# Seven half products in place of eight in the up-projections of a gated convolutional MLP

## The reference, cut to what matters

```
def _conv_ffn(h, w_up, conv_w, conv_b, w_down):
    u = h @ w_up
    up = jnp.pad(u, ((0, 0), (1, 1), (0, 0)))
    u = up[:, :-2] * conv_w[0] + up[:, 1:-1] * conv_w[1] + up[:, 2:] * conv_w[2] + conv_b
    a, v = jnp.split(u, 2, axis=-1)
    return (jax.nn.silu(a) * v) @ w_down
```

## Time and profile before

| | |
|---|---|
| median of 3 runs | 4205.89 us (4193.66 to 4224.21) |
| profiled execution, its own time | 4208.8 us |
| its span, first to last instruction | 4207.0 us |
| share of the span: PE / DVE / ACT / POOL busy | 88% / 52% / 25% / 20% |
| mean granted TensorE clock | 0.953 of 2.4 GHz |
| layer 0's up-projections | 2733.9 to 3188.8 us |
| layer 1's up-projections | 3741.35 to 4045.8 us |

### The profile page before, as it was taken

One profiled execution on the slowest core, in us unless ns is written; L12 is line 12 of the kernel. 1 busy time (PEld: TensorE's weight loads), 2 busy tenths in 40 slices (PEclk: granted clock), 3 DMA queues, 4 the chain that ended last, 5 costly groups with the idle time before them and its releaser, 6 DMA issues.

```text
span 4207.0 us, 52931 instructions
## 1 busy us (share of the span) xinstructions
PE 3699.3 (88%) x21315; PEld 2076.3 (49%) x21315; DVE 2204.5 (52%) x4437; ACT 1050.0 (25%) x2777; POOL 828.1 (20%) x892
## 2 busy tenths in 40 slices
PE   7988898999987998777777777699999998899999
PEld 4555665898855543233332332555554444444444
DVE  4846534787556666776776754623331037533311
ACT  1422221444222333322323322311110022411100
POOL 1034301444201334333333342000000000000000
PEclk8989998899888999999999999899999999999999
DMA  4145520000028999999999998211110111012212
GB/s 165 48 189 226 218 83 8 3 3 3 2 86 305 407 416 420 420 420 420 420 420 420 421 419 355 97 40 48 52 60 35 55 44 60 1 61 80 75 60 75
DMA packets 179573, 751.44 MB, mean 179 GB/s; under 512 B 12215, under 2 KB 74946, under 8 KB 104321
## 3 DMA queue, kind: packets, MB, share of 16 engines
q0 software_dynamic: 77264, 549.79, 31.7%
q1 hardware_dynamic: 101488, 196.16, 13.1%
q10 hardware_dynamic: 576, 2.10, 0.1%
HBM read 745.90 MB, written 2.10 MB: 178 GB/s over the span
## 4 chain that ended last, share of the span: by engine, by line
PE 57%; DMA 19%; DVE 9%; ACT 3%; issue 1%; POOL 0%; DVEq 0%; POOLq 0%; ACTq 0%; SPq 0%
PE bank L104 28%; DMA row<-in_experts,idxs 14%; PE bank L2739 9%; PE bank L2473 6%; DMA wring<-in_experts,idxs 4%; PE bank L2430 2%; PE bank L978 1%; DVE row L2665 1%; PE bank L959 1%; PE bank L1703 1%; PE bank L1677 1%; PE bank L1693 1%; DVE wring L2665 1%; DVE TT L1026 0%; PE bank L2997 0%
## 5 line engine op out<-in xcount | busy, mean ns | idle before, releaser
L2473 PE MATMUL bank<-row,dg 128*128 128x512 f32 x1444 | 692.1, 620 | 208.9 <-ACT dg L2572 208.6
L104 PE MATMUL bank<-h2T,wring 128*128 128x512 f32 (+1 forms) x2112 | 759.3, 522 | 0.0
L2665 DVE CUSTOM_DVE_ANT_0 row<-row,bank 128x1024 f32<-128x1024 f32 x361 | 440.9, 1221 | 305.1 <-DMA row<-in_experts,idxs 285.2
L104 PEld LDWEIGHTS bank<-h2T,wring 128*128 128x128 f32 x2112 | 402.6, 191 | 355.4 <-issue 337.1
L2473 PEld LDWEIGHTS bank<-row,dg 128*128 128x128 f32 x1444 | 272.5, 196 | 593.8 <-issue 580.8
L2723 POOL DMA_INDIRECT row<-in_experts,idxs x361 | 345.8, 958 | 620.1 <-PE bank L2473 553.4
L2739 PE MATMUL bank<-wring,gT 128*128 128x512 f32 x880 | 383.1, 598 | 8.6 <-DVE gT L3137 8.6
L2473 PE MATMUL bank<-wring,dg 128*128 128x512 f32 x604 | 294.3, 621 | 72.7 <-ACT dg L2572 72.6
L3126 DVE TENSOR_SCALAR cv<-pad,fp 128x769 f32<-128x769 f32 (+1 forms) x88 | 54.2, 616 | 509.1 <-ACT pad L3092 509.1
L104 PE MATMUL bank<-hT,wring 128*128 128x256 f32 (+1 forms) x864 | 283.9, 489 | 3.7 <-ACT sq L773 3.0
L2739 PEld LDWEIGHTS bank<-wring,gT 128*128 128x128 f32 x880 | 168.5, 192 | 221.0 <-issue 221.0
(11 more groups left out here) (545 smaller groups left out, 5111.4 us busy)
## 6 DMA issues: line engine op xcount, KB each, us to landing
wring<-in_ada_w SPq DMA_DIRECT2D x36, 2048.0 KB, 8.3
wring<-in_ffn_w_up SPq DMA_DIRECT2D x44, 1024.0 KB, 7.6
wring<-in_peer_w_query SPq DMA_DIRECT2D x16, 1024.0 KB, 9.8
wring<-in_ffn_w_down SPq DMA_DIRECT2D x8, 2048.0 KB, 7.8
wring<-in_w_in SPq DMA_DIRECT2D x7, 2048.0 KB, 8.1
wring<-in_ffn_w_down SPq DMA_DIRECT2D x4, 1536.0 KB, 6.7
wring<-in_attn_w_qkv SPq DMA_DIRECT2D x3, 2048.0 KB, 7.8
row<-in_experts,idxs POOLq DMA_INDIRECT x361, 24.7
```

The costliest lines, as they stand in the source:

```text
L104: ins = e.matmul(out, l, r, start=(start and n == 0), stop=(stop and n == len(pairs) - 1))
L2473: ins = e.matmul(ks[half], self.dg[u % 4], self.places[self.slot[u]][:, 1024 + half * 512:1536 + half * 512], start=(x == 0), stop=(x == 127))
L2665: e.tensor_tensor_reduce(row, row, P.pairs[g % 2], 1.0, 0.0, MUL, ADD, self.dots[:, g % 2, x:x + 1]).then_inc(*V.up("pg_dot", j))
```

## The change

Each pair of parts is treated as a 2 x 2 block product: the two rows of blocks are the `a` and the `v` part, the inner index is split into channel chunks 0 to 3 and 4 to 7, and the tokens are split into two halves (384 and 384 in layer 0, 256 and 256 in layer 1). Eight half products (four chunks over half of the tokens) become seven, with sums ahead of them and behind them (Strassen's scheme in Winograd's form):

- GpSimd forms four sums of weight blocks for each pair, each [128, 4, 128], that is 128 partitions x 512 elements: S3 = A11 - A21, S1 = A21 + A22 (written over A21 in the ring), S2 = S1 - A11, S4 = A12 - S2. S2 and S3 have two buffers, S4 one.
- VectorE forms four sums of token blocks once for each layer (T1 to T4, each [128, 4, 384] or [128, 4, 256]); T2 is written over a part of `h2T`.
- TensorE forms the products in the order 1, 5, 7, 6, 2, 3, 4, each of four matmuls over 384 or 256 tokens, each into a bank of its own.
- ScalarE copies product 1 into the pad of the first part; VectorE adds products 6, 7, 5, 7, 2, 3 and 4 to the pads (one SBUF and one PSUM operand), in 11 instructions in layer 0 (the context's edge cuts four of the adds in two) and 7 in layer 1. The convolution, Silu and `gT` are as before, for a pair at a time. There are two pads for each part of a pair.
- GpSimd issues the four DMAs of the convolution's weights ahead of its `begin`, and clears the four pads (after S2 of pair 0).
- The gate rows are made after the products (`mod_row`), and kept ahead of the last convolution (`keep_row`); their memory is shared with S2 and S3.
- `project` waits, chunk by chunk, only for those `gT` that it reads.

The core of the diff:

```diff
+    def products_pe(self, pe, p):
+        P, name = self.P, self.name
+        wb = self.slots[p // 2][1]
+        a11, a12, a22, s1 = [self.part(wb, p, *rc) for rc in ((0, 0), (0, 1), (1, 1), (1, 0))]
+        for n, lhs, rhs, needs in ((1, a11, self.B11, ()),
+                                   (5, s1, self.T1, (("T1",), ("S1", p))),
+                                   (7, self.S3[p % 2], self.T3, (("T3",), ("S3", p))),
+                                   (6, self.S2[p % 2], self.T2, (("T2",), ("S2", p))),
+                                   (2, a12, self.B21, ()),
+                                   (3, self.S4, self.B22, (("S4", p),)),
+                                   (4, a22, self.T4, (("T4",),))):
+            k = P.bank(pe, name, "P", n, p)
+            for need in needs:
+                pe.wait_ge(*P.at(name, *need))
+            mm(pe.e, k[:, 0:self.n], [(lhs[:, c], rhs[:, c]) for c in range(4)]).then_inc(*self.T.up(name, "P", n, p))
...
     def pe(self, pe):
-        for v, g in enumerate(self.gr):
-            mod_row(pe, P, T_, f"{name}_gate{v}", lambda n: P.modT[1 + self.layer][:, 40 + n, v:v + 1])
...
-                    if self.nctx:
-                        k0 = P.bank(pe, name, "u0", n)
-                        mm(e, k0[:, 0:NC], [(l(c), hT[:, c, 0:NC]) for c in range(8)])
-                    mm(e, k1, [(l(c), hT[:, c, NC:T]) for c in range(8)]).then_inc(*T_.up(name, "up", n))
+            self.products_pe(pe, p)
+            if p % 2:
+                T_.mark("wfree", w)
+        for v, g in enumerate(self.gr):
+            mod_row(pe, P, T_, f"{name}_gate{v}", lambda n: P.modT[1 + self.layer][:, 40 + n, v:v + 1])
...
+    def tokens_dv(self, dv):
+        e, V, name = dv.e, self.V, self.name
+        e.tensor_tensor(self.T1, self.B12, self.B11, SUB).then_inc(*V.up(name, "T1"))
+        e.tensor_tensor(self.T3, self.B22, self.B12, SUB).then_inc(*V.up(name, "T3"))
+        dv.wait_ge(*V.now())
+        e.tensor_tensor(self.T2, self.B22, self.T1, SUB).then_inc(*V.up(name, "T2"))
+        dv.wait_ge(*V.now())
+        e.tensor_tensor(self.T4, self.B21, self.T2, SUB).then_inc(*V.up(name, "T4"))
+
+    def sums_po(self, po, p):
...
+        po.wait_ge(*P.at("wload", w))
+        if p >= 2:
+            po.wait_ge(*P.at(name, "P", 6, p - 2))
+            po.wait_ge(*P.at(name, "S4", p - 2))
+        e.tensor_tensor(self.S3[p % 2], a11, a21, SUB).then_inc(*G.up(name, "S3", p))
+        po.wait_ge(*G.now())
+        e.tensor_tensor(a21, a21, a22, ADD).then_inc(*G.up(name, "S1", p))
+        po.wait_ge(*G.now())
+        e.tensor_tensor(self.S2[p % 2], a21, a11, SUB).then_inc(*G.up(name, "S2", p))
+
+    def last_sum_po(self, po, p):
+        if p >= 1:
+            po.wait_ge(*P.at(name, "P", 3, p - 1))
+        po.wait_ge(*P.at(name, "S2", p))
+        e.tensor_tensor(self.S4, self.part(self.slots[p // 2][1], p, 0, 1), self.S2[p % 2], SUB).then_inc(*G.up(name, "S4", p))
...
+        for p in range(23):
+            if p >= 1:
+                self.second_dv(dv, p - 1)
+            if p == 22:
+                for v, g in enumerate(self.gr):
+                    keep_row(dv, P, V, f"{name}_gate{v}", g)
+            if p >= 1:
+                self.conv_dv(dv, p - 1)
+            if p < 22:
+                self.first_dv(dv, p)
...
@@ project
-            pe.wait_ge(*ready)
+            pe.wait_ge(*ready(k0 + m - 1))
```

More of the change, by code:

```diff
@@ L3020, in __init__ @@
         self.layer, self.nctx = layer, nctx
-        self.gr = [P.mem("gr", 1024) for _ in range(2 if nctx else 1)]
+        self.sums = P.mem("sums", 2048)
+        self.gr = [self.sums[:, v * 1024:v * 1024 + 1024] for v in range(2 if nctx else 1)]
+        pair = [self.sums[:, v * 1024:v * 1024 + 1024].rearrange("p (s c m) -> p s c m", s=2, c=4) for v in range(2)]
+        self.S2, self.S3 = [q[:, 0] for q in pair], [q[:, 1] for q in pair]
         self.gT = P.mem("gT", 22 * T, 22, T)
-        self.fp, self.rows = P.mem("fp", 176), [P.mem("rows", 128) for _ in range(2)]
-        self.pads = [P.mem("pad", 771) for _ in range(2)]
+        self.fp = P.mem("fp", 176)
+        self.pads = [[P.mem("pad", 771)] for _ in range(2)]
         self.spare = P.top
@@ L3027, in __init__ @@
         self.tmp = [P.mem("tmp", 512) for _ in range(2)]
-        self.Lr = [P.flag(f"{name}_rows_landed{n}", 16) for n in range(2)]
+        for q in self.pads:
+            q.append(P.mem("pad", 771))
+        top = P.top
+        n = self.n = T // 2 if nctx else NX // 2
+        t0 = T - 2 * n
+        lo, hi = slice(t0, t0 + n), slice(t0 + n, T)
+        self.B11, self.B12, self.B21, self.B22 = [P.h2T[:, c:c + 4, t] for c in (0, 4) for t in (lo, hi)]
+        P.top = P.spent0
+        self.T4, self.S4 = P.mem("T4", 4 * n, 4, n), P.mem("S4", 512, 4, 128)
+        assert P.top <= 2400
+        P.top = P.spent1
+        self.T1, self.T3 = P.mem("T1", 4 * n, 4, n), P.mem("T3", 4 * n, 4, n)
+        assert P.top <= P.obase + 2048
+        self.T2 = self.B12
+        P.top = ARENA - 256
+        self.rows = [P.mem("rows", 128) for _ in range(2)]
+        P.top = top
+        assert top <= ARENA - 256
+        self.late = slice(770 - n, 770)
+        self.early = [(slice(1, 257), slice(0, 256)), (slice(258, 386), slice(256, 384))] if nctx else [(slice(258, 514), slice(0, 256))]
+        self.slots = {}
+        self.Lr = [P.flag(f"{name}_rows_landed{r}", 16) for r in range(2)]
     def sy(self, sy):
@@ new lines, in first_dv @@
+    def first_dv(self, dv, p):
+        P, V, name = self.P, self.V, self.name
+        row = lambda r: self.pads[r][p % 2]
+        cut = [cs for _, cs in self.early]
+        c11, c21 = [[(row(r)[:, to], cs) for to, cs in self.early] for r in range(2)]
+        whole = [(row(0)[:, self.late], slice(0, self.n))]
+        uc = [(row(0)[:, self.late][:, cs], cs) for cs in cut]
+        dv.wait_ge(*P.at("free", name, "P", 1, p))
+        if p >= 2:
+            dv.wait_ge(*P.at(name, "conv", 2 * p - 3))
+        self.add_dv(dv, p, 6, uc, c11)
+        dv.wait_ge(*V.now())
+        self.add_dv(dv, p, 7, c21, uc, False)
+        dv.wait_ge(*V.now())
+        self.add_dv(dv, p, 5, whole, whole)
+        dv.wait_ge(*V.now())
+        self.add_dv(dv, p, 7, [(row(1)[:, self.late], slice(0, self.n))], whole)
+        self.add_dv(dv, p, 2, c11, c11)
+        dv.wait_ge(*V.now())
+        self.add_dv(dv, p, 3, whole, whole)
@@ L3113, in dv @@
             e.tensor_copy(self.fp[:, 88 * r:88 * r + 88], P.ps(name, "cols", r)[:, 0:88]).then_inc(*V.up("free", name, "cols", r))
[L3114 to L3138, removed]
+        dv.wait_ge(*P.at(name, "pad_zero"))
+        for p in range(23):
+            if p >= 1:
[3 more added lines that the diff above has]
+                    keep_row(dv, P, V, f"{name}_gate{v}", g)
+            if p >= 1:
+                self.conv_dv(dv, p - 1)
+            if p < 22:
+                self.first_dv(dv, p)
         if self.nctx:
```

99 lines of the change are left out of this document (69 added, 30 removed).

## The result

The changed kernel takes 4097.65 us (median of 4 runs, 4094.81 to 4101.14) against 4215.05 us (median of 4 runs, 4193.66 to 4227.36) for the kernel before on the same chip: a ratio of 0.9727, 95% interval 0.9681 to 0.9773. The forecast was 4110, with a range of 4088 to 4138. The profiled execution took 4094.9 us, 113.9 less than that of before; the prediction's sum was 97.2. The median given for experiment 2 leaves out one execution in a slower state (9295.97 us, over twice the others).

The account below looks back on a forecast made before the run. TensorE's stream was taken to bound the kernel. Savings of 89.8 us (stream) and 7.4 (stage ends), together 97.2, off the profiled 4208.8 gave 4111.6, forecast as 4110 us, range 4088 to 4138.

Parts of the forecast that it names:

- TensorE's stream is what bounds both stretches: Both layers' feed-forward stretches: TensorE's instruction stream sets the time, a pair taking 18.10 us in layer 0, 12.18 in layer 1.
- 89.8 us for the stream: TensorE's seven products in place of eight save 55.7 us in layer 0 and 34.1 in layer 1.
- rival D: TensorE's weight loads are not hidden at the narrower width: +100 us and more, about 4210; chance 0.02.
- rival B: TensorE's stream pays for shorter products through added waits and a cold clock: +9 to +20 us, 4119 to 4130; chance 0.11.
- VectorE 11.7 and 8.2 us a pair without contention: VectorE's work a pair in layers 0 and 1, hidden behind TensorE's 18.1 and 12.2 us.
- Two sums take turns with the convolution, 10.3 us in layer 1: Two GpSimd sums of 1.04 us delay VectorE's convolution through the shared port, 8.2 + 2.1 = 10.3 us a pair.
- Rival C: Each GpSimd sum holds VectorE for 1.96 us, layer 1's pair 16.0: slower than before, 4228; chance 0.03.
- GpSimd reads a slot 2 to 4 us before TensorE: Weight ring: GpSimd must read a slot 2 to 4 us earlier; the 7.6 us load stays hidden.
- Rival A: VectorE becomes the bound in layer 1, all four sums holding it, 13.2 us a pair: +22 us, 4132; chance 0.13.
- Fronts: gain 1.1 and 1.4, and 2 lost to the clock: Stage starts, layers 0 and 1: earlier products gain 1.1 and 1.4 us after stalls; a longer cold clock costs 2.
- Backs: gain 3.7 and 3.2: Stage ends, layers 0 and 1: `project` starts on early chunks, only gate rows and copies remain, gaining 3.7 and 3.2 us.
- Sum: Whole kernel: 89.8 us from the stream plus 7.4 from the stage ends, 97.2 us saved.

Follow-up runs that it names:

- experiment 2: Changed kernel, but `project` waits for the last `gT` before its first matmul; 4123.46 us, ratio 0.9761.
- experiment 4: Changed kernel with product 1 of every pair computed twice into its bank, so eight half products; 4196.02 us, ratio 0.9947.
- 7: Changed kernel with the weight sums made by VectorE, GpSimd only clearing the pads; 4101.20 us, ratio 0.9740.
- experiment 3: Changed kernel without GpSimd's four weight sums, products 5, 7, 6 and 3 reading plain weight blocks; 4107.90 us, ratio 0.9740.
- experiment 8: Changed kernel with GpSimd forming S3 and S4 twice and S2 three times, eight instructions a pair; 4149.13 us, ratio 0.9835.
- Experiment 9: Changed kernel with throwaway matmuls filling TensorE's waits ahead of both feed-forward fronts; 4113.44 us, ratio 0.9737.
- experiment 5: Changed kernel with four 128x512 clears added on VectorE behind each pair's `gT`; 4103.48 us, ratio 0.9739.
- experiment 10: Changed kernel with both the weight sums on VectorE and throwaway matmuls ahead of the fronts; 4100.99 us, ratio 0.9706.

## Why the prediction was right

- **TensorE's stream is what bounds both stretches.** Right. TensorE is busy in the whole of both windows; experiment 4 shows a product to be worth its own length, 7 and the first of the loads on VectorE show slack there. The forecast itself was low on the gain by more than its own bounds allowed: 4097.65 lies just below the 4098 to 4120 that it gave 0.68, and inside the wider range.
- **89.8 us for the stream.** Measured 93.0. The term was mis-sized by 3.2 us, in the choice between two ends: the prediction took 217.5 and 323.3 ns; the trace has 215.9 and 322.5. The lower end was the true one. 217.5 came from one short stream, 215.8 from a difference over 43 parts.
- **Weight loads hide behind 216 ns of matmul (rival D).** Right: 842 matmuls and 841 loads of 190 ns in the 181.35 us of 15 pairs, with no gap. By the sentence of the Trainium skill that the prediction tells ("TensorE: Matmul & The Clock Gate", on packing small matmuls) the loads would wait, since their row group is the same; this trace contradicts it at this width too.
- **0 for the waits added to TensorE's queue (rival B).** Right: no idle time and 215.9 ns with a new bank every eight instructions.
- **VectorE 11.7 and 8.2 us a pair without contention.** Right. For layer 1, experiment 3 gives 115.43 / 15 = 7.7 us busy and 15 gaps of 0.036, 8.2. In layer 0 it has 159.23 us busy in 15 pairs, 10.6 a pair, and with 19 gaps 11.3; the changed kernel has 177.37, so contention adds 1.2.
- **Two sums take turns with the convolution, 10.3 us in layer 1.** The mechanism was right, two sums do fall there. The sum of the pair came to 140.65 / 15 + 0.5 = 9.9: the delay over the pair is 1.7 us, not 2.1. Rival C needed 1.96 us for each sum; the largest delay of a convolution instruction beside one sum is 0.88, and even with GpSimd at 92% (experiment 8) layer 1's pair went to 13.1, not to 16.0. The turns in the rows above agree with the exclusive lock of the Trainium skill ("SBUF — State Buffer", "SBUF: two separate sides"), with the price that each blocked instruction ends 0.54 us (VectorE, 512 columns) or 1.13 us (GpSimd) after the other's end.
- **GpSimd reads a slot 2 to 4 us before TensorE.** Wrong, and without effect. S3 of the next pair starts at 3766.57, and TensorE opens that pair at 3778.92: 12.3 us earlier. A slot is freed 24.2 us before TensorE opens it, so the load has some 11.6 us and not 20 before GpSimd needs it; it takes 7.6, and GpSimd never waited for it. GpSimd's sums of 1.27 us, 5.4 a pair, lie in the stated 4.2 to 7.8; its share in layer 0, 29%, is below the stated 35 to 60%.
- **Rival A.** Its mechanism exists and is exactly the wait it named, but its point lies further out: it needs more than 12.1 us a pair on VectorE, and the kernel has 9.9.
- **Fronts: gain 1.1 and 1.4, and 2 lost to the clock.** S1 was ready 5.62 us after the start of T1, as worked out from turns (5.6), though the single turns were 1.12 and 1.62 us in place of 1.04 and 1.77, so that the close agreement is in part luck. The stall of 2.2 us did not appear. Product 1 at 0.50 of the clock used the same time, 2.8 us more than its own. Stall and cold clock lay side by side, where the prediction added them. Measured in layer 0: before, the products started 4.1 us late and lost 0.8 to the clock; after, 0.5 and 2.8, a gain of 1.6. In layer 1: before 4.2 and 2.2, after 0.5 and 2.5 with the wait of 0.57 in it, a gain of 3.4. Experiment 9 is the check: take the cold clock away, and the wait stands in its place.
- **Backs: gain 3.7 and 3.2.** Measured 5.5 and 4.5. Here the step failed that gave the gate rows their old durations, 3.65 and 1.94 us. They had been measured behind idle time, at a granted clock of 0.50; behind a busy stream, at 1.00, they take 1.91 and 1.04.
- **Sum.** The ends gave 1.6 + 3.4 + 5.5 + 4.5 = 15.0 against 7.4, the stream 93.0 against 89.8; 56.8 + 1.6 + 5.5 = 63.9 and 36.2 + 3.4 + 4.5 = 44.1 are the two stretches. Both errors lie on the same side. The remaining 5.9 of the 113.9 lies outside the two stretches, 5.6 of it ahead of the first anchor, a part that moves between executions.

## What to carry to other kernels

When one engine is busy for the whole of a stretch, count its instructions and multiply by the spacing of a long stream of the same width; the cover on the other engines is the thing to test, and adding idle work to them until the bound moves tells how much there is (here 2.6 us a pair fitted on VectorE, and left it without a wait). A duration measured behind idle time on TensorE holds the low clock in it: if the change moves the operation behind a busy stream, take the warm price. At the starts of these stages a slow first product and a wait for an operand overlapped, so they enter the sum as the larger of the two, and curing one only showed the other.

## What the runs showed of the hardware

- A GpSimd tensor_tensor of 1.27 us lengthened a VectorE instruction with two SBUF inputs by 0.88 us in the stream (also the tensor_scalar of the convolution, which reads one tensor, from 0.55 to 1.05 in experiment 5), and was itself lengthened to 1.60. The one that came second ended 0.54 us (VectorE, 512 columns) or 1.13 us (GpSimd) after the other's end. Adds with one input in PSUM stayed at 0.423 and 0.555 us in all of it. At the front, beside VectorE's sums of 1536 elements, GpSimd's went to 2.77 us and VectorE's from 1.76 to 2.82.
- The spacing of float32 matmul instructions followed the columns: 215.9, 322.5 and 429.1 ns for 256, 384 and 512, with one weight load of 190 ns each at all three.
- Filling TensorE's waits with matmuls raised the clock of product 1 from 0.50 to 0.82 in layer 0 and to 1.00 in layer 1. Product 5 then ran at 0.51 behind a wait of 2.47 us (experiment 9, layer 1), and at 1.00 behind waits of 1.42 (its layer 0) and 1.60 (experiment 10).
